# One transformer-style program on one Trainium2 core: feed-forward activation split block by block, last down products by output quarter

## The reference

```python
def rmsnorm(x, g):
    y = xf * lax.rsqrt(jnp.mean(xf * xf, axis=-1, keepdims=True) + EPS)
    return y * g
...
mix = einsum('btc,cd->btd', concat([mix_a, mix_b]), w_out)          # 1024 -> 1024
x = x + rmsnorm(mix, post_mix_g)
h = rmsnorm(x, pre_ffn_g)
u = causal_dwconv(einsum('btd,df->btf', h, ffn_w_up), ffn_conv_w)   # 1024 -> 2 x 2816, 3 taps
gate, val = split(u, 2, axis=-1)
y = einsum('btf,fd->btd', silu(gate) * val, ffn_w_down)             # 2816 -> 1024
x = x + rmsnorm(y, post_ffn_g)
```

## Time and profile before

| what | value |
|---|---|
| median of 3 runs | 1445.15 us |
| the profiled execution's own time | 1446.88 us |
| its span, first to last instruction | 1445.1 us |
| TensorE matmul busy | 1359.8 us (94%), 7356 instructions |
| VectorE / ScalarE / GpSimd busy | 438.7 / 331.5 / 57.6 us |
| mean granted TensorE clock | 0.983 of full speed |
| chain that ended last, by engine | TensorE 79%, DMA 11%, VectorE 6%, ScalarE 2% |

### The profile page before, as it was taken

The page is one execution under the profiler, slowest core; times in us unless marked ns, Lnnn a source line. Parts: engine busy times, 40 slices in busy tenths (PEclk is TensorE's granted clock), DMA queues, the critical chain, the costliest instruction groups (busy, mean ns, idle before and its releaser), DMA issues.

```text
span 1445.1 us, 16969 instructions
## 1 busy us (share of the span) xinstructions
PE 1359.8 (94%) x7356; PEld 727.0 (50%) x7356; DVE 438.7 (30%) x727; ACT 331.5 (23%) x532; POOL 57.6 (4%) x72
## 2 busy tenths in 40 slices
PE   7998999999879999999999999999989878999997
PEld 6996333333223333333333333332349874799975
DVE  4555111001010010010010001100157563677754
ACT  4440101101011011011011000110145421565543
POOL 1001000000000000000000000000000000033310
PEclk9998999999979999999999999999999999999999
DMA  9747899999999999999999999999965400654530
GB/s 376 274 185 289 364 431 430 430 431 430 430 416 430 431 429 431 431 430 431 430 431 430 430 430 431 430 431 431 429 254 204 146 30 0 247 191 176 177 115 30
DMA packets 43738, 483.12 MB, mean 334 GB/s; under 512 B 4652, under 2 KB 4704, under 8 KB 13072
## 3 DMA queue, kind: packets, MB, share of 16 engines
q1 hardware_dynamic: 41824, 476.58, 79.3%
q0 software_dynamic: 1840, 5.44, 1.1%
HBM read 480.94 MB, written 1.06 MB: 334 GB/s over the span
## 4 chain that ended last, share of the span: by engine, by line
PE 79%; DMA 11%; DVE 6%; issue 2%; ACT 2%; SPq 0%; ACTq 0%; DVEq 0%
PE bank L732 25%; PE bank L562 18%; PE bank L740 14%; DMA ring<-in_moe_w_gate_up 10%; PE bank L998 4%; PE bank L752 3%; PE bank L705 3%; PE bank L544 3%; PE bank L724 2%; PE bank L957 2%; PE bank L651 2%; PE bank L918 1%; ACT w_hi L1047 1%; DMA ring<-in_a_w_in 1%; DVE ring L1658 1%
## 5 line engine op out<-in xcount | busy, mean ns | idle before, releaser
L732 PE MATMUL bank<-ring,arena 128*64 128x512 f32 x2048 | 451.9, 597 | 14.1 <-DMA ring<-in_moe_w_gate_up 14.1
L732 PEld LDWEIGHTS bank<-ring,arena 128*64 128x64 f32 x2048 | 143.2, 137 | 321.4 <-issue 291.1
L740 PE MATMUL bank<-ring,arena 128*64 128x512 f32 x1024 | 226.8, 595 | 0.9 <-ACT arena L1149 0.9
L1532 DVE TENSOR_SCALAR arena<-bank 128x512 f32<-128x512 f32 x32 | 22.1, 692 | 669.5 <-PE bank L732 669.5
L562 PE MATMUL bank<-x_hi,w_hi 128*128 128x256 f32 x640 | 185.3, 289 | 13.6 <-DVE w_lo L1348 10.4
L562 PE MATMUL bank<-x_lo,w_hi 128*128 128x256 f32 x640 | 183.0, 286 | 0.0
L562 PE MATMUL bank<-x_hi,w_lo 128*128 128x256 f32 x640 | 182.8, 286 | 0.0
L1334 DVE TENSOR_TENSOR w_lo<-ring,w_hi 128x2048 fp32r<-128x2048 f32 x61 | 139.6, 2291 | 115.0 <-ACT w_hi L1047 115.0
L1047 ACT CAST w_hi<-ring 128x2048 fp32r<-128x2048 f32 x61 | 116.4, 1908 | 117.7 <-PE bank L562 92.9
L740 PEld LDWEIGHTS bank<-ring,arena 128*64 128x64 f32 x1024 | 70.7, 137 | 135.7 <-issue 127.9
L1143 ACT ACTIVATE arena<-arena 128x512 f32<-128x512 f32 x32 | 20.2, 630 | 502.7 <-DVE arena L1532 502.7
(11 more groups left out here) (267 smaller groups left out, 1140.2 us busy)
## 6 DMA issues: line engine op xcount, KB each, us to landing
ring<-in_moe_w_gate_up SPq DMA_DIRECT2D x128, 2048.0 KB, 25.5
ring<-in_moe_w_down SPq DMA_DIRECT2D x64, 2048.0 KB, 27.3
ring<-in_ffn_w_up SPq DMA_DIRECT2D x22, 1024.0 KB, 4.8
ring<-in_w_in SPq DMA_DIRECT2D x14, 1024.0 KB, 6.5
ring<-in_a_w_in SPq DMA_DIRECT2D x11, 1024.0 KB, 19.0
ring<-in_ffn_w_down SPq DMA_DIRECT2D x11, 1024.0 KB, 4.9
ring<-in_a_w_out SPq DMA_DIRECT2D x2, 2048.0 KB, 20.7
ring<-in_w_out SPq DMA_DIRECT2D x2, 2048.0 KB, 8.1
```

What stands on the lines that cost most here:

```text
L732: last = mm(bank[q // 2][half * 64:half * 64 + 64, :], chunk(xeT, c), w[:, c % 2, q * 512:(q + 1) * 512], start=False, stop=c == KC - 1)
L740: last = mm(bank[3][half * 64:half * 64 + 64, :], chunk(actT, c), w[:, c % 4, half * 512:(half + 1) * 512], start=c == 0, stop=c == KC - 1)
```

## The change

1. The activation is split one block at a time, during the up loop, from a double buffer `a32` into `a_hi` and `a_lo`, which have room for all 22 blocks and are apart from `x_hi` and `x_lo`.
2. ScalarE computes silu in place of sigmoid, and GpSimd does one product per block in place of two. It now waits for `a_lo` of block f - 2, whose place in `a32` it writes.
3. The first 8 down pieces run as before. The last 3 are held together, and run four times: for each token tile and column half all three pieces in a row (18 matmuls), then that quarter's sums can start.
4. The root chain: squares start per half; the sums are added with eps times D in one instruction, and ScalarE's Ln divides by D; VectorE multiplies bank by gain while ScalarE works on the root, and multiplies by the root and adds the residual in one instruction per half. `refine` takes three steps in place of four wherever a root is for one column (12 of 13 uses).
5. The output leaves in four DMAs of 256 KB in place of two of 512 KB.
6. The split of piece `UP + 1` is moved ahead of the mix part's sums.

```diff
 # SyncE
-for t in range(NT):
-    sp.wait_ge(y_done, t + 1)
-    sp.dma_start(out[t * P:(t + 1) * P, :], y_out[:, t, :]).then_inc(out_done, 16)
+for n in range(2 * NT):
+    t, cols = n // 2, slice(n % 2 * 512, (n % 2 + 1) * 512)
+    sp.wait_ge(y_done, n + 1)
+    sp.dma_start(out[t * P:(t + 1) * P, cols], y_out[:, t, cols]).then_inc(out_done, 16)
 # GpSimd
 for f in range(FB):
-    pool.wait_ge(cv_ready, f + 1)
-    pool.tensor_tensor(aT[:, f, :], y[:, 1, :], y[:, 0, :], ALU.mult).then_inc(a_prod, 1)
-    pool.wait_ge(a_prod, f + 1)
     pool.wait_ge(up_sig, f + 1)
-    pool.tensor_tensor(aT[:, f, :], aT[:, f, :], sgt[:, f % 2, :], ALU.mult).then_inc(a_ready, 1)
+    if f >= 2:
+        pool.wait_ge(a_lo_ready, f - 1)
+    pool.tensor_tensor(a32[:, f % 2, :], cv[:, f % 2, T:2 * T], sgt[:, f % 2, :], ALU.mult).then_inc(a_ready, 1)
 # TensorE
-pe.wait_ge(x3_ready, NT)
+pe.wait_ge(x3_ready, 2 * NT)
...
-for p in range(FB // 2):
-    ...
-    if p < FB // 2 - 1:
-        for c in (2 * p, 2 * p + 1):
-            for t in range(NT):
-                last = down(c, t)
-        last.then_inc(piece_used, 1)
-    else:
-        for t in range(NT):
-            down(2 * p, t)
-            down(2 * p + 1, t).then_inc(down_ps, 1)
+together = FB // 2 - SPLITS
+for p in range(together):
+    pe.wait_ge(lo_ready, DOWN + p + 1)
+    pe.wait_ge(a_lo_ready, 2 * p + 2)
+    ...
+    last.then_inc(piece_used, 1)
+for t in range(NT):
+    for g in range(2):
+        for p in range(together, FB // 2):
+            pe.wait_ge(lo_ready, DOWN + p + 1)
+            pe.wait_ge(a_lo_ready, 2 * p + 2)
+            for c in (2 * p, 2 * p + 1):
+                last = down(c, t, g)
+        last.then_inc(down_ps, 1)
 # ScalarE
-link(activate(inv_root[:, c:c + k], variance[:, c:c + k], ACT.Ln))
+link(activate(inv_root[:, c:c + k], variance[:, c:c + k], ACT.Ln, scale=1.0 / summed[n]))
...
+split_hi(UP + 1)
 for t in range(NT):
-    act.wait_ge(mix_ps, 2 * t + 2)
-    squares_of(t, (2 + 2 * t, 3 + 2 * t), mix_sq)
+    squares_of(t, (2 + 2 * t, 3 + 2 * t), mix_ps, squares_at, mix_sq)
...
-split_hi(UP + 1)
...
-    activate(sgt[:, f % 2, :], cv[:, f % 2, 0:T], ACT.Sigmoid).then_inc(up_sig, 1)
+    activate(sgt[:, f % 2, :], cv[:, f % 2, 0:T], ACT.Silu).then_inc(up_sig, 1)
...
+def split_a_hi(f):
+    act.wait_ge(a_ready, f + 1)
+    copy(a_hi[:, f, :], a32[:, f % 2, :]).then_inc(a_hi_ready, 1)
...
 for f in range(FB):
     act.wait_ge(up_ps, f + 1)
-    if f == FB - 1:
-        split_a_hi(0)
     split_hi(UP + f + SPLITS)
...
     if f >= 1:
         sigmoid_gate(f - 1)
+    if f >= 2:
+        split_a_hi(f - 2)
 sigmoid_gate(FB - 1)
+split_a_hi(FB - 2)
+split_hi(DOWN + SPLITS)
+split_a_hi(FB - 1)
+for p in range(SPLITS + 1, FB // 2):
+    split_hi(DOWN + p)
 # VectorE: refine
-link(tt(w, y, y, ALU.mult))
-link(tt(w, w, v, ALU.mult))
+link(stt(w, y, v, y, ALU.mult, ALU.mult))
 # VectorE: rms_residual
-link(tt(sq_sum[:, t:t + 1], sums[0], sums[1], ALU.add))
-r = root(n, sq_sum[:, t:t + 1], 1.0 / D, RMS_EPS)
-for g in range(2):
-    last = stt(dst[:, t, cols], bank[banks[g]][:, :], r, gain[:, cols], ALU.mult, ALU.mult)
-link(last)
-tt(dst[:, t, :], dst[:, t, :], base[:, t, :], ALU.add).then_inc(ready, 1)
+for g, cols in enumerate(halves):
+    dve.wait_ge(done, 2 * t + g + 1)
+    if g:
+        ts(variance[:, c:c + 1], ss2[:, 2 * t:2 * t + 1], ss2[:, 2 * t + 1:2 * t + 2], D * RMS_EPS,
+           ALU.add, ALU.add).then_inc(var_ready, 1)
+    last = tt(dst[:, t, cols], bank[banks[g]][:, :], gain[:, cols], ALU.mult)
+link(last)
+r = refine(n)
+for cols in halves:
+    stt(dst[:, t, cols], dst[:, t, cols], r, base[:, t, cols], ALU.mult, ALU.add).then_inc(ready, 1)
 # VectorE: up loop
 for f in range(FB):
-    if f == FB - 1:
-        split_a_lo(0)
+    if f >= 3:
+        split_a_lo(f - 3)
     split_lo(UP + f + SPLITS)
```

More of the change, by code:

```diff
@@ L140, in build @@
         roots = [(n, 1) for n in range(6)] + [(6, 2 * HG)] + [(n + 7, 1) for n in range(7, 13)]
+        summed = [D if n >= 7 else 1 for n in range(13)]
         variance, inv_root, newton = at(13612, 24), at(13636, 24), at(13660, 24)
@@ L242, in build @@
         x3 = at(4112, NT, D)
-        aT = scratch(0, FB, T)
+        a_hi = sb("a_hi", [P, FB, T], SCRATCH * SLOT, f32r)
+        a_lo = [sb(n, [P, k, T], SLOTS * SLOT + start, f32r) for n, k, start in (("a_lo0", 16, 0), ("a_lo1", FB - 16, 6160))]
+        a32 = at(7696, 2, T)
         up_sb = scratch(5632, 2, 2 * (T + 2))
@@ L246, in build, with a_lo_of @@
         sgt = at(10400, 2, T)
-        y_out = at(2048, NT, D)
+        y_out = at(8208, NT, D)
+        def a_lo_of(f):
+            return a_lo[f // 16][:, f % 16, :]
         first_in, rest_in = sem("first_in"), sem("rest_in")
@@ L304, in build @@
                                                   sem("a_ready"))
[L305 removed]
+        cv_ready, cv_tap = sem("cv_ready"), sem("cv_tap")
         down_ps, down_sq, y_done, out_done = sem("down_ps"), sem("down_sq"), sem("y_done"), sem("out_done")
@@ L988, in _, with down @@
                 last.then_inc(up_ps, 1)
-            def down(c, t):
+            def down(c, t, g):
                 n = (DOWN + c // 2) % SPLITS
-                hi, lo = (v[:, n, (c % 2) * D:(c % 2 + 1) * D] for v in (w_hi, w_lo))
+                hi, lo = (v[:, n, (c % 2) * D + g * 512:(c % 2) * D + (g + 1) * 512] for v in (w_hi, w_lo))
                 part = slice(t * P, (t + 1) * P)
-                a_hi, a_lo = x_hi[:, c % KC, part], x_lo[:, c % KC, part]
-                for g in range(2):
[L996 to L1000, removed]
@@ L1002, in _ @@
[L1002 to L1013 removed]
+                a, b = a_hi[:, c, part], a_lo_of(c)[:, part]
@@ new lines, in down @@
+                for k, (x, w) in enumerate(((a, hi), (a, lo), (b, hi))):
+                    last = mm(bank[2 * t + g][:, :], x, w, start=c == 0 and k == 0, stop=c == FB - 1 and k == 2)
+                return last
+            together = FB // 2 - SPLITS
[7 more added lines that the diff above has]
+                last.then_inc(piece_used, 1)
@@ L1312, in _ @@
                     sigmoid_gate(f - 1)
-            split_a_hi(1)
+                if f >= 2:
+                    split_a_hi(f - 2)
             sigmoid_gate(FB - 1)
-            for p in range(2, FB // 2):
-                if p + 1 < FB // 2:
-                    split_hi(DOWN + p + 1)
-                split_a_hi(p)
+            split_a_hi(FB - 2)
[3 more added lines that the diff above has]
+                split_hi(DOWN + p)
             nc.scalar.preload_act_table_set(log_exp)
             for t in range(NT):
-                act.wait_ge(down_ps, t + 1)
-                squares_of(t, (2 * t, 2 * t + 1), down_sq)
+                squares_of(t, (2 * t, 2 * t + 1), down_ps, lambda start, size: scratch(5632 + start, size), down_sq)
                 rough_root(11 + t)
```

62 lines of the change are left out of this document (28 added, 34 removed).

## The result

| | before | changed |
|---|---|---|
| median of the runs | 1445.13 us (4 runs, 1444.72 to 1446.24) | 1435.29 us (4 runs, 1433.74 to 1436.48) |
| profiled execution's own time, span | 1446.88, 1445.1 | 1436.48, 1434.7 |
| mean granted TensorE clock | 0.983 | 0.986 |

The ratio is 0.9929, with a 95% interval of 0.9917 to 0.9941: 9.8 us faster. The forecast was 1435.8, by 9.35 us. To see where the time went I cut both traces at the same events, which are found in either: the start of the last experts' group, the first input product of the second block, the first and the second mix group, the first up product, the last up product, the first squares behind the last matmul, the end of the span.

The account below looks back on a forecast made before the run. TensorE's products were taken to bound the kernel, with gains only where TensorE stands still; 0.75 + 2.5 + 1.4 + 0.6 + 4.1 = 9.35 us takes 1445.15 to 1435.8, own range 1434.4 to 1437, 8 in 10 1434.3 to 1439.0.

Parts of the forecast that it names:

- Shorter root: Second block's start: four roots lose one refining step of 0.20 us each, 0.75 us gained, bounds 0 and 0.8.
- Mix to up: From mix product to up products: wait for x3 gone, up begins 2.5 us earlier, bounds 1.3 and 2.9.
- The clock: Start of up: with TensorE's pauses shortened, 1.4 of 1.8 us lost to the lower clock return, bounds 0 and 1.8.
- Rival A: Clock does not profit: fall stays, 1437.2 us, or with a second fall behind the stall in down 1438.8; chance 14%.
- The up loop: Up loop: extra rounding and VectorE's 0.35 to 0.69 us subtraction per block hidden by TensorE's 5.84 us; no change.
- Between up and down: Between up and down: 2.4 us of waits go, a new 1.8 us stall comes; net gain 0.6, bounds 0 and 1.0.
- Behind the last matmul: Last matmul to end: last quarter's shorter chain and smaller DMA take 6.0 us, gain 4.1, bounds 3.2 and 4.8.
- Rival B: Unread matmuls and DMA keep the ends: first 0.75 hidden, up only 1.3 earlier, DMA still 2.6; gain 6.8, 1438.4 us; 11%.

Follow-up runs that it names:

- the repeat: The changed kernel run again unaltered, beside the kernel before: 1434.99 us (6 runs), ratio 0.9934.
- the split alone: The changed kernel with only the block-by-block activation split, silu and single GpSimd product kept, the rest as before: 1444.05 us, ratio 0.9989 to the kernel before.
- the first four kernels: Changed kernel with only the activation split kept, last piece by token tile, two pieces held, or one: 1444.05, 1435.68, 1433.83 and 1430.88 us.

## Why the prediction was right, point by point

**Shorter root: right in kind, a quarter too large.** 0.75 was forecast, 0.52 came; the term took a step as 0.20 saved, and the fused step takes 0.26 in place of two that take 0.39 together. Four roots give 4 x 0.13 = 0.52, and the kernel with four steps gives it back (0.54).

**Mix to up: right in size, wrong in its account.** 2.5 forecast, 2.57 measured, with the unread matmuls late next, as predicted; the kernel with two of them fewer shows it, as its up begins another 1.41 earlier. Wrong was the share of the move of UP + 1. The prediction counted it as what lets the start of up follow the transposes closely. The kernel with the late split shows the same 24.36. The 0.1 us that it has to spare there says that the move may be needed once fewer unread products are issued; that pair wasn't run.

**The clock: right in size, wrong in its cause.** 1.4 forecast, 1.36 measured. The prediction spoke of both pauses and read "only transposes between" them; the earlier trace rows show six unread matmuls of 2.84 us ahead of the transposes. In the one trace in which the first pause was filled, the fall came all the same, so the second one is enough. The Trainium skill, in "TensorE: Matmul & The Clock Gate", section "HAM oscillation — how this bites in real kernels", says that waits between bursts of matmuls put the array back to the slow clock, and the waits it describes are longer than the two pauses here. So it doesn't tell which of these cost the clock, and the removed ones could not be priced by it. In the runs the clock falls behind the pauses of 1.76 to 1.86 and of 2.17 us, and stays at 1.00 behind those of 1.60, of 1.61 (the stall in down) and of 2.15 us at 1174.43. Rival A, a fall behind the new stall, did not come; its price there should have been 1438.6 (1437.2 + 1.4), not 1438.8.

**The up loop: right.** Nothing was forecast and nothing was lost: the 0.435 of VectorE lies within the 0.35 to 0.69 forecast, GpSimd waits for silu and not for a_lo, and TensorE's block takes 127.17 / 22 = 5.78 us (5.84 before, with the slow start). ScalarE's silu takes 0.44 us, as its sigmoid did, with a single table load of 1.28 us for all 22, as the order had said. What the prediction had missed is harmless: GpSimd's one product, 1.27 us, takes nearly two thirds of the 0.78 and 1.21 of the two before (means of 22).

**Between up and down: 0.6 forecast, 0.37 measured.** Both pauses went (2.25, forecast 2.4), and the stall came at the predicted place, 12 matmuls into the last 72, ended by VectorE's weight split (1.88, forecast 1.8). The sum was right and the thought behind it too short: a stall that I forecast at 1.8 us should have led to the question whether the three pieces are worth it. Measured, they are worth 0.66 against the order by tile, and cost 1.88.

**Behind the last matmul: 4.1 forecast, 3.74 measured.** The DMA landed in 2.0 us, as taken. The two halves with the residual take 1.41 instead of 1.35, and the last root starts its steps 0.33 us late, behind bank times gain. The chain accounts for 1.65 of the gain and the DMA for 0.56. Holding the pieces gives 0.66. Undone together, these cost more than their sum: 10.26 in the kernel with the split alone, where the sum would be 6.39 + 1.65 + 0.56 + 0.66 = 9.26. There the first tile's longer chain holds VectorE until 1434.9, though the second tile's squares are done at 1433.3; before, it is the same.

**What the total hides.** The touched stretches explain 8.56 of the 9.8 us that the first medians show, and of 10.1 in the repeat. Rival B's 6.8 did not come: the first root's steps were not hidden, up began 2.57 us earlier and the DMA took less. The other 1.3 to 1.5 us lie in stretches in which no instruction was altered, between 1078 and 1215 us, where the granted clock falls or doesn't. Between the mix groups the time is 17.8 or 16.1 us, and ahead of them 120.2 to 121.2, or 117.2. The same 32 matmuls of the first mix group, behind the same pause of 2.98 us, take 15.70 us before and 14.00 changed:

```profile
1199.25 15.70 PE L957 MATMUL bank<-ring 128*128 128x512 f32 x32 [2.98 <-DVE ring L1712]
```

```profile
1198.58 14.00 PE L964 MATMUL bank<-ring 128*128 128x512 f32 x32 [2.98 <-DVE ring L1721]
```

That is the whole 1.7 us of the third row, and it shows that one and the same pause costs the clock in one execution and not in another. All four traces with a four-step root ahead of that stretch (before, the split alone, four steps alone, before with a filled pause) have the longer value in both. Of the ten with three steps six have the shorter one between the mix groups, and four in the stretch ahead. But of the 14 executions of the kernel before that stand beside the first four kernels, two took 1440.8 and 1440.9 us at a mean granted clock of 0.987, and the other twelve 1443.9 to 1447.7 at 0.981 to 0.984. No trace of the two was kept; the short stretches (1.7 and 3.1 us less) would account for them, so the kernel before most likely has them too. Whether they come more often when the stretch starts 0.5 us earlier, these runs don't settle, and the agreement of 1435.8 with 1435.3 is in part luck: without it the sum of my terms, 9.35, would have been 0.8 too high.

## What to carry to other kernels

When two edits can each remove the same wait, run each of them without the other before crediting either: here the earlier weight split and the shorter chain each shortened the pause ahead of up to 0.9 us, and with one of them in place the other was worth nothing more for it. When a reorder makes a stall that you can compute beforehand, weigh it at once against the smaller reorder: two pieces held instead of three keep the short end and have no stall (66.6 us from up's end, against 68.5). And filler work that keeps TensorE busy must shrink when the chain it covers shrinks.

## What the runs showed of the hardware that was not expected

A fused step on one column (128x1, three inputs, two operations) takes 0.22 us and 0.26 from start to start, against 0.15 to 0.16 and 0.19 for a plain one; fusing two of them saves 0.13 us, not one whole step. An output DMA lands after 2.6 us with 512 KB and after 2.0 us with 256 KB. TensorE's clock level in a stretch can differ between two executions of the same code by 3.1 us of time in 120, so a difference of 1 us in a total says little, while stretches between fixed events repeat to 0.1 us where the clock is equal. A pause of 2.98 us ahead of the mix products costs 1.7 us of clock in one execution and nothing in another.
